# PEER encoder layer, gate tables: half of the dense tokens added into DRAM by indirect DMAs, the other half made four tokens beside each u tile

## What is computed

```
qp = (h @ w_query).reshape(B, T, 8, 2, 128)
s = einsum('bthcd,hcnd->bthcn', qp, sub_keys)
top_s, top_i = top_k(s, 16)
cand = top_s[..., 0, :, None] + top_s[..., 1, None, :]      # 256 candidates
best_s, pos = top_k(cand, 16)
gate = softmax(best_s)                                       # 8 heads x 16 experts for each token
a = gelu(h . u[expert]);  out = sum(a * gate * v[expert])
```

## Time and profile before

| | us |
|---|---|
| three timed runs, median | 1901.35 |
| lowest, highest | 1891.34, 1902.92 |
| the profiled execution, its own time | 1894.8 |
| its span, first to last instruction | 1893.0 |
| PE, DVE, ACT, POOL busy | 1753.9, 1106.8, 780.9, 931.1 |
| mean granted TensorE clock, share of full | 0.967 |

### The profile page before, as it was taken

The page is one execution under the profiler, slowest core; times in us unless marked ns, Lnnn a source line. Parts: engine busy times, 40 slices in busy tenths (PEclk is TensorE's granted clock), DMA queues, the critical chain, the costliest instruction groups (busy, mean ns, idle before and its releaser), DMA issues. The chain is left out here.

```text
span 1893.0 us, 32097 instructions
## 1 busy us (share of the span) xinstructions
PE 1753.9 (93%) x11464; PEld 1446.5 (76%) x11464; DVE 1106.8 (58%) x2245; ACT 780.9 (41%) x1268; POOL 931.1 (49%) x743
## 2 busy tenths in 40 slices
PE   7979867879999986888998999999999999999997
PEld 5867734448998886888998778787777778787875
DVE  2662578235769999995444455454545554555454
ACT  5333326434333343444444344444444444444443
POOL 3473711006678783000003767666666667666763
PEclk9989959989999997999999999999999999999999
DMA  5212151014555453566778899999999999999996
GB/s 181 101 45 67 16 157 56 1 55 158 170 170 158 130 170 117 173 248 231 230 227 275 321 332 325 341 335 334 327 330 348 327 333 325 345 329 334 326 335 242
DMA packets 166004, 427.22 MB, mean 226 GB/s; under 512 B 23456, under 2 KB 74400, under 8 KB 165280
## 3 DMA queue, kind: packets, MB, share of 16 engines
q1 hardware_dynamic: 118992, 273.20, 43.1%
q0 software_dynamic: 45056, 134.38, 19.6%
q10 hardware_dynamic: 1872, 18.56, 2.4%
HBM read 390.02 MB, written 36.04 MB: 225 GB/s over the span
## 5 line engine op out<-in xcount | busy, mean ns | idle before, releaser
L1756 POOL DMA_INDIRECT rows<-in_peer_v,row_i x252 | 258.1, 1024 | 209.4 <-PE psum L1950 142.0
L1740 POOL DMA_INDIRECT spot<-acts_first,spot_i x256 | 296.1, 1157 | 83.5 <-issue 77.4
L1923 PE MATMUL psum<-h2hi,u_hi 128*128 128x256 f32 x1024 | 293.3, 286 | 2.8 <-PEq L1400 2.8
L1923 PE MATMUL psum<-h2lo,u_hi 128*128 128x256 f32 x1024 | 290.0, 283 | 0.0
L1923 PE MATMUL psum<-h2hi,u_lo 128*128 128x256 f32 x1024 | 289.4, 283 | 0.0
L1923 PEld LDWEIGHTS psum<-h2hi,u_hi 128*128 128x128 f32 x1024 | 194.8, 190 | 58.0 <-issue 32.3
L1933 PE MATMUL psum<-v_hi,w_hi 128*128 128x512 f32 x512 | 202.6, 396 | 2.0 <-DVE w_lo L1835 2.0
L1933 PE MATMUL psum<-v_hi,w_lo 128*128 128x512 f32 x512 | 203.4, 397 | 0.0
L1933 PE MATMUL psum<-v_lo,w_hi 128*128 128x512 f32 x512 | 202.7, 396 | 0.0
L1818 DVE TENSOR_TENSOR u_lo<-u_raw,u_hi 128x1024 fp32r<-128x1024 f32 x126 | 154.4, 1226 | 78.9 <-ACT u_hi L1774 78.9
L1829 DVE TENSOR_TENSOR wgt<-gel,g_in 128x256 f32<-128x256 f32 x128 | 54.6, 426 | 247.7 <-ACT gel L1784 247.7
(11 more groups left out here) (247 smaller groups left out, 3913.9 us busy)
## 6 DMA issues: line engine op xcount, KB each, us to landing
u_raw<-in_peer_u SPq DMA_DIRECT2D x256, 512.0 KB, 4.4
v_raw<-in_peer_v SPq DMA_DIRECT2D x128, 512.0 KB, 6.6
acts_first<-gel SPq DMA_DIRECT2D x128, 128.0 KB, 2.0
gates<-chunk ACTq DMA_DIRECT2D x4, 4096.0 KB, 12.4
g_in<-gates SPq DMA_DIRECT2D x64, 256.0 KB, 2.9
wring<-in_w_in SPq DMA_DIRECT2D x24, 512.0 KB, 3.6
wq_raw<-in_w_query SPq DMA_DIRECT2D x16, 512.0 KB, 5.9
w_out<-in_w_out SPq DMA_DIRECT2D x1, 4096.0 KB, 18.4
```

Of the source, the lines that this page charges most:

```text
L1740: pool.indirect_dma_start(spot[:, t:t + 1], None, spots, bass.IndirectOffsetOnAxis(ap=spot_i[:, t:t + 1], axis=0)).then_inc(s_spot, 16)
L1756: pool.indirect_dma_start(rows[:, slot, :], None, values, bass.IndirectOffsetOnAxis(ap=row_i[:, t:t + 1], axis=0)).then_inc(s_rows[q % PER ...
L1923: last = pe.matmul(psum[:, ACTS + s % 2, 0:DENSE], a[:, s % 2, k, :], b[:, k, GATHERED:T], start=(k == 0 and a is u_hi and b is h2hi), sto ...
```

## The change

Of the 256 dense tokens the tables of 128 (384 to 511, `TABLED`) are still made by products, four tokens beside each of the first 32 u tiles. `hot_j`, `hot_i` and PSUM have a slot for each of four tiles; ACT copies one bank and, after 16 tiles, stores 4 MB, so there are two such stores.

The gates of the other 128 (256 to 383, `SPREAD`) go into DRAM one by one. In the routing POOL clears 4 KB a partition (`blank`, a part of `chosen`, L1100) and SP issues 16 stores of 512 KB of it, 8 MB, into the first two chunks of `gates`, behind `load_w(0)` and `load_w(1)` and ahead of its loop. A third small load on ACT's queue brings the partition's number, and four small DVE instructions between `reduce_picks(7)` and the sum of the gates (L1333, L1334) make `gate_at`, the place of each gate; one more, last of all, makes `gate_of`. In `build_gates` POOL issues for each head 16 indirect DMAs of 128 elements of 4 bytes with an add at the destination, and waits for the 16 before it goes to the next head.

In `build_gates` ACT now does `split_ahead` ahead of `gelu`, in all turns, and its first eight turns are written out.

```diff
 # build_routing
+        blank = chosen[:, 0:2, :].rearrange("p j t -> p (j t)")
+        BLANKS = P * CHUNK // (2 * T)
@@ sync
             load_w(0)
             load_w(1)
+            sp.wait_ge(s_blank, 1)
+            for c in range(P // CHUNK):
+                for i in range(BLANKS):
+                    w = P // BLANKS
+                    sp.dma_start(gates[c, :, i * w:(i + 1) * w, :].rearrange("j i t -> j (i t)"), blank).then_inc(s_zero, 16)
             for n in range(EARLY_ROUTING + 4):
@@ scalar
+            act.dma_start(place_at[:, 0:1], dram["iota"][0:1, :].rearrange("a p -> p a")).then_inc(s_in, 16)
...
+            act.wait_ge(s_zero, 16 * BLANKS * (P // CHUNK))
             for j in range(3):
                 act.wait_ge(s_turn, j + 1)
@@ gpsimd
+            pool.memset(blank, 0.0).then_inc(s_blank, 1)
             rest_w(0)
@@ vector
             reduce_picks(PH - 1)
+            steps.inc(dve.tensor_scalar(place_at[:, 1:2], place_at[:, 0:1], float(CHUNK), float(P * P * CHUNK - CHUNK),
+                                        ALU.is_ge, ALU.mult))
+            dve.wait_ge(s_top, steps.n)
+            steps.inc(dve.tensor_tensor(place_at[:, 0:1], place_at[:, 0:1], place_at[:, 1:2], ALU.add))
+            dve.wait_ge(s_red, 2 * PH)
+            steps.inc(dve.scalar_tensor_tensor(flat_at[:], found[:, 1, SPREAD, :, :], float(P), found[:, 0, SPREAD, :, :],
+                                               ALU.mult, ALU.add))
+            dve.wait_ge(s_top, steps.n)
+            steps.inc(dve.tensor_scalar(gate_at[:], flat_at[:], float(CHUNK), place_at[:, 0:1], ALU.mult, ALU.add))
             dve.wait_ge(s_gexp, 1)
...
+            dve.tensor_tensor(gate_of[:], best[:, :, SPREAD, :], ginv[:, :, SPREAD].unsqueeze(2).to_broadcast([P, PH, TOPK]),
+                              ALU.mult).then_inc(s_g, 1)
 # build_gates
+        @block.gpsimd
+        def _(pool):
+            cells = gates.rearrange("c j i (t a) -> (c j i t) a", a=1)
+            for h in range(PH):
+                if h:
+                    pool.wait_ge(s_added, 16 * TOPK * h)
+                for s in range(TOPK):
+                    pool.indirect_dma_start(cells, bass.IndirectOffsetOnAxis(ap=gate_at[:, h, s:s + 1], axis=0),
+                                            gate_of[:, h, s:s + 1], None, compute_op=ALU.add).then_inc(s_added, 16)
+            pool.wait_ge(s_added, 16 * TOPK * PH)
@@ vector
-                wait(dve, s_prod, (batch - 1) * QUADS)
+                wait(dve, s_prod, m - USLOTS + 1)
+                tokens = bass.ds(m * FOUR + FIRST, FOUR)
...
+                for s in range(FOUR):
...
@@ tensor
+            def products(m, e):
+                pe.wait_ge(s_hot, m + 1)
+                wait(pe, s_moved, m - USLOTS + 1)
+                for s in range(FOUR):
+                    last = pe.matmul(psum[:, e, s * P:(s + 1) * P], hot_j[:, e, s, :], hot_i[:, e, s, :], start=True, stop=True)
+                last.then_inc(s_prod, 1)
@@ scalar
+            def move(turn, e):
+                m, half = turn * USLOTS + e, turn // HALF
+                start = m * FOUR % CHUNK
+                act.wait_ge(s_prod, m + 1)
+                act.copy(chunk[:, half, :, start:start + FOUR],
+                         psum[:, e, :].rearrange("p (s i) -> p i s", s=FOUR)).then_inc(s_moved, 1)
+                if start + FOUR == CHUNK:
+                    act.wait_ge(s_moved, m + 1)
+                    act.dma_start(gates[(FIRST - GATHERED) // CHUNK + half, :, :, :].rearrange("j i t -> j (i t)"),
+                                  chunk[:, half, :, :].rearrange("p i t -> p (i t)")).then_inc(s_st[half], 16)
+            for turn in range(BESIDE):
+                for e in range(USLOTS):
+                    split_ahead(turn, e)
+                    gelu(turn, e)
+                    move(turn, e)
             with act.Fori(BESIDE, TURNS - 1) as it:
                 for e in range(USLOTS):
+                    split_ahead(it, e)
                     gelu(it, e)
-                    split_ahead(it, e)
```

More of the change, by code:

```diff
@@ L62 @@
 CHUNK = 64
+SPREAD = GATHERED // P
+TABLED = P
 CHOSEN_BANKS = (4, 5, 0)
@@ L1409, in build_gates @@
         u_hi2, u_lo2 = keep["u_hi2"], keep["u_lo2"]
+        gate_at, gate_of = keep["gate_at"], keep["gate_of"]
         keep["picked"] = nc.dram_tensor("picked", [P, 3, GATHERED], F32).ap()
@@ L1519, in activations, with beside @@
                 last.then_inc(s_act, 1)
-            def body(it):
-                for b in range(BATCHES):
-                    batch = it * BATCHES + b
-                    activations(batch, b % USLOTS)
-                    pe.wait_ge(s_gated, batch + 1)
-                    pe.wait_ge(s_hot_j, batch + 1)
-                    for q in range(QUADS):
-                        wait(pe, s_moved, (batch - 1) * QUADS + q + 1)
-                        for s in range(4):
-                            last = pe.matmul(psum[:, q, s * P:(s + 1) * P], hot_j[:, b % 2, q * 4 + s, :],
-                                             hot_i[:, b % 2, q * 4 + s, :], start=True, stop=True)
-                        last.then_inc(s_prod, 1)
-            body(0)
-            with pe.Fori(1, ITERS) as it:
-                body(it)
+            def products(m, e):
[4 more added lines that the diff above has]
+                last.then_inc(s_prod, 1)
+            def beside(turn):
+                for e in range(USLOTS):
+                    activations(turn * USLOTS + e, e)
+                    products(turn * USLOTS + e, e)
+            beside(0)
+            with pe.Fori(1, BESIDE) as it:
+                beside(it)
             with pe.Fori(BESIDE, TURNS) as it:
@@ L1557, in gelu @@
                 act.activation(gel[:, e % 2, 0:GATHERED], psum[:, 6 + e % 2, 0:GATHERED], ACT.Gelu).then_inc(s_gel, 1)
-            def body(it):
-                for b in range(BATCHES):
-                    batch, half = it * BATCHES + b, b // HALF
-                    gelu(it * 2 + b // USLOTS, b % USLOTS)
-                    split_ahead(it * 2 + b // USLOTS, b % USLOTS)
-                    if b % HALF == 0:
-                        wait(act, s_st[half], it * 16)
-                    for q in range(QUADS):
-                        act.wait_ge(s_prod, batch * QUADS + q + 1)
-                        start = (b % HALF) * BATCH + q * 4
-                        act.copy(chunk[:, half, :, start:start + 4],
-                                 psum[:, q, :].rearrange("p (s i) -> p i s", s=4)).then_inc(s_moved, 1)
-                    if b % HALF == HALF - 1:
-                        act.wait_ge(s_moved, (batch + 1) * QUADS)
-                        act.dma_start(gates[bass.ds(it * 2 + half, 1), :, :, :].rearrange("c j i t -> j (c i) t"),
-                                      chunk[:, half, :, :]).then_inc(s_st[half], 16)
```

83 lines of the change are left out of this document (41 added, 42 removed).

## The result

The changed kernel is slower: 1936.43 us (median of 4 runs, 1932.49 to 1938.17) against 1902.13 (4 runs), ratio 1.0168 with the interval 1.0137 to 1.0199. The forecast was 1881 with a range up to 1950 and the range of its own case up to 1893; what came is rival 2, the dear adds, for which 1932 had been worked out at a pitch (the time from the start of one add to that of the next) of 1.86 us. The pitch was 2.03 us and the waits between the groups shorter than put, so that this number comes near is in part luck.

What follows compares the result with a forecast made beforehand. DVE's batches were taken to bound the gates stage, then PE and POOL together. Gates stage -39.5, zeros +18.2, end of routing +0.9 gave -20.4 us: 1881 us against the median 1901.35, range 1862 to 1950.

Steps and rivals of the forecast that it cites:

- rival 2: Gates stage: the chain of adds is dear, 1932 us at a pitch of 1.86; chance 0.35.
- its own case: Whole kernel: the forecast of 1881 us itself, with its own range of 1868 to 1893; chance 0.42.
- What bounded the stage: Gates stage before the change: 16 batches at DVE's 7.8 to 8.0 us each, the 48 tiles behind them at PE's pace.
- Part 1: Gates stage on PE: four tokens beside each of 32 tiles, 3.96 us a tile; 42 us earlier.
- Part 2: Gates stage on POOL: the 128 adds take 231 us, ending 3 us after PE alone; stage 39.5 us shorter.
- X: Gates stage: time of POOL's chain of adds, put at 231 us, between 159 and 335.
- The bound from above: Gates stage: the chain of adds priced at the longest gather, 1.97 + 0.30 us, gives 335 us.
- The rule on the ports: Gates stage: DVE's one-input `hot_i` holds the port pair shared with GpSimd, blocking POOL up to 34 us.
- Part 3: Start of the routing: 8 MB of zeros delay the third weight load; PE, POOL and DVE slip by 18.2 us.
- part 4: End of the routing: four small DVE operations on the path to the sum of gates, 0.9 us.
- Rival 3: Gates stage: u loads set the tail, 32 tiles cost 7 to 10 us more, about 1888 us; chance 0.13.

Runs made afterwards that it cites:

- e1: Changed kernel without all 128 adds, so the gates of tokens 256 to 383 stay zero: 1873.31 us, ratio 0.9835 to the kernel before.
- e3: Changed kernel with its 128 indirect DMAs writing plainly, without the add: 1874.33 us, ratio 0.9843 to the kernel before.
- e8: Changed kernel with DVE's rest of u as a one-input copy, not a two-input subtraction: 1920.68 us in a single run.
- e2: Changed kernel with the 16 stores of zeros issued one beside each u tile from the ninth on: 1916.61 us, ratio 1.0068 to before.
- e9: e5 with ACT doing the gelu ahead of the cast, as the kernel before did: 1919.44 us, ratio 1.0068 to the kernel before.
- e5: Changed kernel without adds, zeros or index arithmetic; all 256 tokens tabled, four beside each of 64 tiles: 1897.95 us, ratio 0.9956 to before.
- e11: Against the changed kernel: no adds or zeros, 256 tokens tabled, eight beside each of 32 tiles, cast before gelu: 1898.76 us, ratio 0.9966 to before.

## Why the prediction was wrong

The direction was wrong, and one term made it so.

- **What bounded the stage.** Right: DVE with sixteen tokens a batch. With four beside a tile PE sets the pace, 3.76 us where 3.96 was worked out.
- **Part 1, PE's part.** 228.7 us forecast. Without adds it was 228.7 (e1), with them 233.4. The tiles were shorter than put, 32 x 3.77 in place of 32 x 3.96, 6 us, and the two stores dearer, about 12 us in place of 7, so the exact agreement is luck.
- **Part 2, the chain of adds: the step that failed.** I took the price of an add from the gathers' mean, 1.157 us and a pitch of 1.457, because no row was nearer. An add took 1.693 us in the mean, at a pitch of 2.03. X was 285.8 us from the start of the first add to the end of the last, and not 231. The adds themselves took 216.7 us where 148.1 was put, 68.6 more; between them went 42.9 where 36 was put, 6.9 more; the seven waits took 26.2 where eight were put at 46.8, 20.6 less (the landing of the last group lies in the 2.9 us behind X). So the price of an add is the error, and the smaller waits, six of the seven 1.7 to 3.2 us and not 5.85, hid a part of it. Of the 216.7 us, 18.3 are DVE work that adds started under; 128 x 1.55 = 198.4 are the adds alone. With the add taken out and nothing else changed (e3), the mean is 1.17 us, the borrowed price: what failed is the step from a gather to an add. The bound from above (335 us) held. Rival 2 had this mechanism and was thought less likely than the forecast. That its 1932 at a pitch of 1.86 comes so near is in part luck: by its own sum the pitch of 2.03 gives X = 304 and 1954 us.
- **The rule on the ports.** Up to 34 us were given to DVE's `hot_i`. Measured are 18.3 us of delay: 16.9 under the subtraction, 1.2 under `hot_j` and 0.3 under `hot_i`. Only one add started under a `hot_i`: two adds (3.7 us) nearly fill a tile of 3.77, so they fell at the same place in tile after tile. In e8 fifteen started under one, and all fifteen together lost 0.7 us.
- **Part 3, the zeros.** Right: 15.5 us of slip and 2.7 for the clock were forecast, ACT's wait was 14.1 us, PE's 14.8, and with part 4 the routing grew by 17.6 where 19.1 was worked out; e2 takes 19 us back. That a ring is consumed in order, as the Trainium skill says ("DMA: Bandwidth & Descriptors", Queues, rings and completion order), fits: the third weight load, issued at 435.5 behind sixteen stores, landed at 450.6, 1.3 us after the last of them. Issuing the sixteen took SP 14.35 us, and not 7; it was hidden all the same. That DVE's 28.07 us wait doesn't absorb it was right to the last digit.
- **Behind the stage.** The sum foresaw no long wait of PE at the end, and so nothing for the clock after it; the wait was 55.6 us. The granted clock of the next stage's first ten microseconds was 0.68 in place of 0.94, and the experts took 1.9 us more.
- **Part 4.** The four small instructions start 0.78 us before the reduction they stand ahead of; 0.9 was put.
- **Rival 3.** Its mechanism was seen only from one side: the cast ahead of the gelu makes ACT wait for loads (68 us in the stage). In the tail a load landed in 3.9 us in the median, and the last 26 tiles took 3.05 us each in place of 2.88, 4.5 us in all; 7 to 10 were put, and here POOL's chain covered them. But this order also opens a loop over DVE, and is worth 24 us where all tiles have tokens (e9 against e5).

Not tried: the adds without the waits between the heads, since two heads can add to the same cell.

## What to carry to other kernels

A new kind of instruction on an engine that was idle is not free because the engine was idle: work out the whole chain at a price per piece, and where the price is borrowed from a neighbour, find the price at which the sum turns (here 1.62 us, only 11% above the borrowed one) before giving chances. Bulk stores belong in pieces beside the loop whose loads share the DMA engines, and not ahead of it or in one block: that alone was worth 19 us for the zeros and 22 us for the tables. And when an engine is relieved, look for loops through the program order of a third engine; swapping two lines on ACT was worth 24 us where every tile had four tokens, and 4 where half of them had eight and the four big stores took most of it back.

## What the runs showed of the hardware that I hadn't expected

- An indirect DMA with an add costs POOL 1.54 us at least, the same without the add 0.95. With 64 elements in place of 128 it is 1.41: most of it doesn't depend on the elements.
- An add that starts under a DVE instruction, a two-input subtraction or a one-input copy, ends 1.42 to 1.46 us after that instruction does. A subtraction that starts under a running add costs neither anything; a copy that does is held until 1.54 us into the add, or holds the add by up to 0.31 us.
- Small adds into DRAM land fast: six of the seven waits after sixteen adds were 1.7 to 3.2 us, and one 11.7, in the stretch of a 4 MB store, while the gathers before showed 4.85.
- Eight MB of stores from SBUF moved at 419 GB/s in the ten microseconds looked at, with every engine idle, and a load of 512 KB issued behind them landed only when they were done.
- After each 4 MB store of e11 PE stood still for some us, and then the granted clock was 0.50 for 6 us or more; over the stage it was 0.95 in the mean, and 0.99 with the stores in pieces.
